# The MLP of a decoder layer as block products: two phases instead of one interleaved stream

## The reference

```python
D_MODEL = 2048; SEQ = 512; D_FF = 4 * D_MODEL
hf = rms_norm(x, norm_mlp[l])
x = x + jnp.square(jax.nn.relu(hf @ w_up[l])) @ w_down[l]
return rms_norm(x, norm_final)
```

## Time and profile before

| | |
|---|---|
| time, median of 3 runs | 2840.79 us (2839.5 to 2841.35) |
| profiled execution, its own time | 2839.88 us |
| its span, first to last instruction | 2838.2 us |
| mean granted TensorE clock | 0.998 |
| instructions | 33822 |

### The profile page before, as it was taken

How to read it: one execution, slowest core, us unless ns; L and a number is a source line. 1 busy time by engine, 2 the same in 40 slices (tenths; PEclk the granted TensorE clock), 3 DMA queues, 4 the chain that set the end, 5 groups by cost and what they waited for, 6 DMA issues and landing times.

```text
span 2838.2 us, 33822 instructions
## 1 busy us (share of the span) xinstructions
PE 2808.7 (99%) x12777; PEld 2321.5 (82%) x12777; DVE 1597.4 (56%) x2058; ACT 1012.1 (36%) x1370; POOL 403.7 (14%) x254
## 2 busy tenths in 40 slices
PE   8999999999999999999999999999999999999998
PEld 7888888888788888888878888888888888888886
DVE  5222245454335556532344577776777777767776
ACT  6222234343232223322344333334333344333334
POOL 1000000000000001000000322332233223313330
PEclk9999999999999999999999999999999999999999
DMA  7323232332333232543212233233223322332232
GB/s 269 104 93 100 89 104 103 103 103 104 104 119 104 74 111 97 190 165 104 89 60 87 77 119 103 91 104 118 90 88 117 118 84 93 118 118 77 101 119 104
DMA packets 132034, 306.27 MB, mean 108 GB/s; under 512 B 7561, under 2 KB 7674, under 8 KB 129530
## 3 DMA queue, kind: packets, MB, share of 16 engines
q1 hardware_dynamic: 130522, 294.80, 31.0%
q10 hardware_dynamic: 1440, 10.49, 0.9%
HBM read 290.58 MB, written 14.68 MB: 108 GB/s over the span
## 4 chain that ended last, share of the span: by engine, by line
PE 97%; DVE 1%; ACT 1%; issue 0%; DMA 0%; SPq 0%; POOL 0%; POOLq 0%; DVEq 0%; ACTq 0%
PE acc L1668 16%; PE acc L1670 16%; PE acc L1669 16%; PE acc L1994 8%; PE acc L1993 8%; PE acc L1992 8%; PE aux L2012 7%; PE aux L2014 7%; PE aux L2016 7%; PE aux L1689 1%; PE aux L1779 1%; PE aux L1762 0%; PE aux L1761 0%; PE aux L1771 0%; PE acc L2034 0%
## 5 line engine op out<-in xcount | busy, mean ns | idle before, releaser
L1013 DVE TENSOR_TENSOR wlo<-raw,whi 128x2048 fp32r<-128x2048 f32 x128 | 293.3, 2291 | 490.9 <-ACT whi L610 489.8
L1668 PE MATMUL acc<-act_hi,whi 128*128 128x512 f32 x1088 | 432.4, 397 | 0.5 <-DVE act_lo L1017 0.5
L1670 PE MATMUL acc<-act_hi,wlo 128*128 128x512 f32 x1088 | 425.0, 391 | 0.0
L1669 PE MATMUL acc<-act_lo,whi 128*128 128x512 f32 x1088 | 424.1, 390 | 0.0
L1446 DVE TENSOR_TENSOR flo<-wide,fhi 128x1024 fp32r<-128x1024 f32 x188 | 257.7, 1372 | 253.2 <-ACT fhi L884 253.2
L610 ACT ACTIVATE whi<-raw 128x2048 fp32r<-128x2048 f32 x128 | 244.5, 1910 | 435.7 <-PE acc L1670 427.4
L1992 PE MATMUL acc<-act_hi,fhi 128*128 128x512 f32 x1024 | 398.7, 389 | 0.0
L1994 PE MATMUL acc<-act_hi,flo 128*128 128x512 f32 x1024 | 398.4, 389 | 0.0
L1993 PE MATMUL acc<-act_lo,fhi 128*128 128x512 f32 x1024 | 398.4, 389 | 0.0
L884 ACT ACTIVATE fhi<-wide 128x1024 fp32r<-128x1024 f32 x188 | 199.4, 1061 | 525.0 <-PE acc L1994 364.8
L2012 PE MATMUL aux<-fhi,P_hi 128*128 128x512 f32 x840 | 326.8, 389 | 0.2 <-DVE xs L1505 0.2
(11 more groups left out here) (313 smaller groups left out, 4159.8 us busy)
## 6 DMA issues: line engine op xcount, KB each, us to landing
raw<-in_w_in SPq DMA_DIRECT2D x80, 1024.0 KB, 5.1
raw<-in_w_up SPq DMA_DIRECT2D x64, 1024.0 KB, 5.3
wide<-in_w_down SPq DMA_DIRECT2D x64, 1024.0 KB, 5.2
raw<-in_w_out SPq DMA_DIRECT2D x16, 1024.0 KB, 5.1
gates_scratch<-gate_out ACTq DMA_DIRECT2D x10, 1024.0 KB, 3.9
raw<-in_w_ckv SPq DMA_DIRECT2D x8, 1024.0 KB, 11.5
xs<-in_x SPq DMA_DIRECT2D x8, 1024.0 KB, 12.8
raw<-in_w_attn_br SPq DMA_DIRECT2D x8, 1024.0 KB, 8.2
```

The source lines that it names most:

```text
L1013: nc.vector.tensor_tensor(wlo[n % 2][:], raw[n % 4][:], whi[n % 2][:].bitcast(F32), ALU.subtract).then_inc(lo_ready, 1)
L1668: nc.tensor.matmul(dst, s_hi, v_hi, start=first, stop=False)
L1669: nc.tensor.matmul(dst, s_hi, v_lo, start=False, stop=False)
L1670: ins = nc.tensor.matmul(dst, s_lo, v_hi, start=False, stop=last)
```

## The change

The MLP is made in two phases, each of blocks with 14 units (`UNITS`), two units per product and seven products per block.

* **Up phase**, 16 blocks (`N_UP`) of 512 features. The 2x2 block product is over halves of 1024 input features, halves of 256 output features and halves of 256 tokens. A unit is 24 matmuls with **256** tokens moving, and a block is 336. The weight mixes are made by POOL, **eight** per block of 128x1024 (`up_mixes`). The input-side sums are made once, ahead of and within block 0 (`mlp_input`, `input_sum`, `low_lo`, `sum_lo`). Products are gathered in PSUM; ACT reads three partial ones out (`product_read`), DVE adds and squares (`hidden`), ACT relus the last (`last_read`), DVE squares it and makes the four sums of the down projection's left operands (`hidden_sum`).
* The seven left operands of a block are split (`operand_hi` on ACT, `operand_lo` on DVE) into three staging tiles and stored to DRAM by SP (`hid_scratch`), 0.5 MB each. All of it is done while the next block's units run.
* **Down phase**, 16 blocks: blocks over 1024 feature rows and 1024 output columns. A unit is 12 matmuls of 512 columns, two units per product. The left operands come back from DRAM, 1 MB per product, double-buffered; eight POOL mixes per block (`down_mixes`). The last block is 8 plain units with 192 matmuls.
* The residual `xs` is stored to DRAM ahead of the MLP and read back into `x_half` at the end of the up phase, since its space is used in between.

Units in all: up 16 x 14 = 224 and down 15 x 14 + 8 = 218, where there were 128 up and 218 down units before. An up unit has 24 matmuls as before, each with half the columns.

The core of the diff:

```diff
-WITH_UP = ("P1", "U", "P2", "P6", "U", "P7", "P5", "U", "P4", "P3", "U")
+UNITS = 14
 RING = 4
+N_UP = 16
+N_BLOCKS = 32
+OPERAND_POS = {"P1": 0, "P4": 1, "P2": 2, "C12": 3, "P5": 4, "P6": 5, "P7": 6, "P3": 8}
...
+        def load_up(slot, b, ready, count):
+            k, f = slot % 2, slot // 2
+            column = (b.first // 2) * 1024 + f * 512 + (b.first % 2) * 256
+            src = w_up_v[:, 8 * k:8 * k + 8, ds(b.turn * (b.per * 512) + column, 256)]
+            sp.wait_ge(ready, count)
...
+        def loads_after_up(b, load):
+            load(0, b.next(), unit_lo, b.of(UNITS, 8))
+            load(1, b.next(), mix_w_ready, b.of(8, 8))
+        def later_loads_after_up(b, load):
+            load(2, b.next(), unit_lo, b.of(UNITS, 10))
+            load(3, b.next(), unit_lo, b.of(UNITS, 12))
...
+        def up_mixes(b):
+            for u in range(2):
+                pool.wait_ge(unit_lo, b.of(UNITS, u + 1))
+                pool.wait_ge(raw_loaded[2], b.of(16, 512 + 16))
+                mixed(nc.gpsimd.tensor_tensor(half_slot(0, u), half_slot(0, u), half_slot(2, u), ALU.subtract))
+                pool.wait_ge(raw_loaded[3], b.of(16, 512 + 16))
+                pool.wait_ge(mix_w_ready, b.of(8, 2 * u + 1))
+                mixed(nc.gpsimd.tensor_tensor(mix[u][:], half_slot(3, u), half_slot(0, u), ALU.subtract))
+            for u in range(2):
+                mixed(nc.gpsimd.tensor_tensor(half_slot(2, u), half_slot(2, u), half_slot(3, u), ALU.add))
+            for u in range(2):
+                pool.wait_ge(unit_lo, b.of(UNITS, 4 + u + 1))
+                pool.wait_ge(mix_w_ready, b.of(8, 4))
+                mixed(nc.gpsimd.tensor_tensor(mix[u][:], half_slot(1, u), mix[u][:], ALU.subtract))
...
+        def before_unit(b, n):
+            if n == 1:
+                hidden(b, "C21")
+            if n == 3:
+                hidden_last(b)
+                hidden_sum(b, "S1")
+                hidden_sum(b, "S2")
+        def behind_unit(b, n):
+            for name in operand_list(b):
+                if OPERAND_POS[name] == n:
+                    operand_lo(b, name)
+            if n == 3:
+                hidden_sum(b, "S3")
+            if n == 5:
+                hidden_sum(b, "S4")
...
+            for m in range(2):
+                bank = up_bank(b, name)[:, 256 * m:256 * (m + 1)]
+                for i in range(4):
+                    k = 4 * u + i
+                    nc.tensor.matmul(bank, w_hi[:, i, cols(m)], x_hi[:, k, :], start=name in UP_FRESH and n % 2 == 0 and m == 0 and i == 0,
+                                     stop=False, skip_group_check=True)
+                    nc.tensor.matmul(bank, w_hi[:, i, cols(m)], x_lo[:, k, :], start=False, stop=False, skip_group_check=True)
+                    ins = nc.tensor.matmul(bank, w_lo[:, i, cols(m)], x_hi[:, k, :], start=False, stop=u == 1 and i == 3,
+                                           skip_group_check=True)
```

More of the change, by code:

```diff
@@ new lines, in down_block, with next_side @@
+        def down_block(b):
+            d = b.first - N_UP
+            sides_free = d % 2 and (not isinstance(b.turn, int) or b.of(1) < N_BLOCKS - 4)
+            i = (d // 2) % 2
+            q = ds(b.turn * 2 + (d // 2 + 2), 1) if sides_free else None
+            def next_side(pi):
+                if sides_free:
+                    load_side(i, q, PRODUCTS[pi], b.of(UNITS, 2 * pi + 2))
+            next_side(0)
+            next_side(1)
+            for slot, lo, pi in ((1, 8, 2), (0, 10, 3), (2, 12, 4), (3, 14, 5)):
+                load_down(slot, b.next(), unit_lo, b.of(UNITS, lo))
+                next_side(pi)
+            next_side(6)
@@ new lines, in _ @@
+        first = Block_no(0, 2, 0)
+        for slot in range(4):
+            load_up(slot, first, lo_ready, G_FF - 3 + slot)
+            for j in {2: (0,), 3: (1, 2, 3)}.get(slot, ()):
+                for m in range(4):
+                    sp.wait_ge(bank_free[m], freed(B_CO + j, m))
+                sp.dma_start(x2_dram[:, :, cols(j, BLK)], xs[:, :, cols(j, BLK)]).then_inc(x2_stored, 16)
+        for p in range(2):
+            up_block(Block_no(0, 2, p))
+        with sp.Fori(1, N_UP // 2 - 1) as t:
+            for p in range(2):
+                up_block(Block_no(t, 2, p))
@@ new lines, in down_block @@
+        def down_block(b):
+            first = isinstance(b.turn, int) and b.of(1) == N_UP
+            chunk = Block_no(0, 2, N_UP - 1)
+            for n in range(UNITS):
+                if first:
+                    before_unit(chunk, n)
+                elif n in (1, 3):
+                    land(b.next(-1), {1: "P4", 3: "P3"}[n])
+                if n in (5, 7, 9, 11, 13):
+                    land(b, PRODUCTS[(n - 5) // 2])
+                unit_split_lo(b, n, True)
+                if first:
+                    behind_unit(chunk, n)
@@ L1611, in left_gain @@
+        last = Block_no(0, 2, N_BLOCKS - 1)
+        for n in range(8):
+            if n in (1, 3):
+                land(Block_no(0, 2, N_BLOCKS - 2), {1: "P4", 3: "P3"}[n])
+            dve.wait_ge(unit_hi, last.of(UNITS, n + 1))
+            nc.vector.tensor_tensor(flo[ring(last, n)][:], half_slot(n // 2, n % 2), fhi[ring(last, n)][:].bitcast(F32),
+                                    ALU.subtract).then_inc(unit_lo, 1)
         def left_gain(m):
             if m == 0:
-                dve.wait_ge(fin_loaded, 16)
+                dve.wait_ge(fin_loaded, 32)
@@ new lines, in down_unit @@
+        def down_unit(b, n):
+            name, u, d = PRODUCTS[n // 2], n % 2, b.first - N_UP
+            i_ = (d // 2) % 2
+            pe.wait_ge(unit_lo, b.of(UNITS, n + 1))
+            if u == 0:
+                if d % 2 == 0 and name in ("P1", "P5"):
+                    h, loads = (0, 4) if name == "P1" else (1, 3)
+                    pe.wait_ge(side_loaded[i_][h], b.turn * (b.per * 4 * loads) + (d // 4 + 1) * 16 * loads)
+                p = PRODUCTS.index(name)
+                if isinstance(b.turn, int) and b.of(1) == N_UP + 1 and p < 2:
+                    pe.wait_ge(dve_read, 4 * N_UP)
+                if p >= 2:
+                    pe.wait_ge(pair_free, b.of(7, p - 1 - 7 * N_UP))
+            a_hi, a_lo = sides[i_][name][:, 0], sides[i_][name][:, 1]
+            w_hi, w_lo = (f[ring(b, n)][:].rearrange("p (k n) -> p k n", k=2) for f in (fhi, flo))
+            for m, bank in enumerate(bank_pair(d % 2, name)):
@@ L2053, in _, with plain_side @@
[L2053 to L2065 removed]
+        def plain_side(m, k):
+            t = sides[1][{(0, 0): "P1", (0, 1): "P2", (1, 1): "P4"}[m // 2, k // 4]] if (m // 2, k // 4) != (1, 0) else side_c12
+            return t[:, 0, k % 4, cols(m % 2)], t[:, 1, k % 4, cols(m % 2)]
```

929 lines of the change are left out of this document (502 added, 427 removed).

## The result

The kernel after takes **2991.5 us** (median of 4 runs, 2990.97 to 2993.32), the kernel before 2840.25 (4 runs, 2839.5 to 2841.35): 1.0533 times as long, 95% interval 1.0515 to 1.0552. It is slower, by 151 us where 84 had been forecast; 2991.5 lies inside the range of 2862 to 3000, near its upper end.

What follows compares the result with a forecast made beforehand. PE's matmuls were taken to bound the kernel before; POOL and DVE delaying each other would make PE wait after the change. Terms -51 + 106 + 20 + 10 = +85 on 2839.9 gave 2924 us, range 2862 to 3000.

Steps and rivals of the forecast that it cites:

- matmuls, 0.120 us apart: Up phase: 5376 matmuls of 256 columns at 0.120 us replace 3072 of 512 at 0.2267, -51.3 us.
- 15 up blocks: Steady up blocks: PE waits 7.1 us per block of 47.4 us; +106 us, bounds +68 to +146.
- start, block 0: Block 0: input differences on DVE alternate with POOL's mixes and delay PE; +20 us, bounds 10 to 30.
- between the phases: Last up to first down block: +6 us for DVE and POOL, +4 for queued stores; +10 us.
- the next thirteen: Down blocks: DVE's lead covers the delay from POOL; 0 us, bounds 0 to 1.5 per block, 21 in all.
- turns: DVE operations with two SBUF inputs and POOL mixes alternate, each waiting out the other; 44 us per up block.
- Squares: DVE's squares in up blocks: counted as waiting for POOL; if free, a block is 0.4 us shorter, 6 in all.
- covered by little: Down blocks: over eight mixes DVE falls back 5.0 us against a lead of 5.7, so no cost.
- Rival 3: Up phase: slot 3's weights land too late for POOL's second mix; 4 us per block, +60, 2984 us; chance 0.14.

Runs made afterwards that it cites:

- narrow: The kernel after with POOL's mixes cut to one column in all blocks but the first, mixed weights left out of the result: 2827.8 us.
- fill: The kernel after with one column of each mix computed and the other 1023 filled with a constant, in all blocks: 2816.1 us.
- queues: The kernel after with down-block weight loads issued ahead of side loads, and x2 and P3 loads behind the first operands' stores between phases: 2973.9 us.
- spread: The kernel after with the fifth to eighth POOL mix of an up block made to wait for later units' splits, same work: 2964.5 us.
- late0: The kernel after with POOL's first mixes held back until block 0's last low input part is done: 3001.7 us.
- combo2: The kernel after with mixes on DVE, SP's loads reordered, block 0's first mixes and sums behind all x2 additions: 2820.35 us, 0.9928 of the kernel before.

## Why the prediction came out as it did

Where the 152 us of the profiled executions (2992.0 against 2839.9) lie, by the prediction's own terms; each is the stretch less what PE wants there at full clock:

| term | forecast | measured |
|---|---|---|
| matmuls, 0.120 us apart | -51.3 | -51.3 |
| 15 up blocks | +106 | +125.5 (15 x 8.37) |
| start, block 0 | +20 | +24 |
| between the phases: the first down block | +10 | +24.5 |
| the next thirteen | 0 | +28.5 |
| sum | +85 | +151 |

So the time came out 67 us above the forecast: 19.5 of them in the up blocks, 4 at the start, 14.5 between the phases, 28.5 in the down blocks. Two terms lie outside their own bounds, the step between the phases (24.5 against at most 21) and the down blocks (28.5 against at most 21); that the total stayed inside the range is partly luck, since the up blocks (at most 146) and the start (at most 30) stayed under theirs. The measured terms add up to within 1 us of the 152, which is closer than they are sharp (the last block of seven products, 1.8 us too long, is in none of them); the start is the least sharp of them (17.9 us idle in 65.9, and about 6 by matmuls at a clock of 0.87; the 48.03 us busy would be some 42 at full clock).

**Right, and shown: turns.** The mechanism is the one forecast: `narrow` cuts the mixes to one column and `fill` keeps their writes without the reads, and in both the up blocks fall to 40.3 us and DVE from 44.2 to 28.2. The 20.9 us from unit 0's split to unit 3's had been worked out as 20.4, and unit 7's split came 13.2 us later (20.9 to 34.1) against 13.0. That the 44 us of turns and DVE's busy 44.2 are the same number is partly luck: the first is 25 of DVE's own and 19 of POOL's, the second 28 of DVE's own and 16 spent beside mixes. Adding instructions up in their order from rows of a kernel that never waited was good to half a microsecond in 21.

**Matmuls.** The 256-column ones come 0.120 us apart, as the earlier trace rows said. By the formula of the Trainium skill, "TensorE: Matmul & The Clock Gate", Back-to-back issue gap, it would be 0.109 and 25 us more of gain; the trace does not agree. That section of the Trainium skill gives the formula for an isolated matmul, which the prediction left out, and about 131 ns at 512 columns for a stream with weight loads; the earlier trace rows have 226.7, so neither holds for this kernel.

**Squares.** They wait too (2.02 us at 1623.56, where one that meets no mix takes 0.69). So the rule of the Trainium skill, "SBUF — State Buffer", Who interferes with whom, that any DVE instruction with two SBUF inputs waits, agrees with the trace, and so does its other half, that POOL instructions which only write don't contend (`fill`).

**Mis-sized: the up block**, 8.4 us for 7.1. Of the 1.3 us too few, 0.5 are hand-overs up to unit 3's split, 0.2 those from there to unit 7's and 0.2 to 0.3 PE's short delays around unit 7: together they make the block of 48.4 us, where 47.4 had been forecast. The other 0.3 are PE's clock. No step of the prediction asked what the 6 us wait, which it had forecast, does to the matmuls behind it. The first 1.7 us of that loss fall where PE would otherwise wait for unit 7; only where the low clock lasts longer does the block grow. The trace bears this out over the 15 blocks: with 14 to 19 slow steps a block takes 48.4 or 48.5 us, with 20 or 21 it takes 48.5 or 48.6, with 26 to 28 it takes 49.2 to 49.4.

**Mis-sized: the step between the phases**, 24.5 us for 10. The place and both causes were named. In `narrow` the first down block takes 56.4 us and the second catches up with 34.0, 14.2 us lost in both; so by this difference about 10 us of the 24.5 are turns, where 6 had been said, and 14 are transfers and what waits for them, where 4 had been said. Stores were said to queue behind the reads, but the length was not worked out. Ten microseconds of the wait, in the kernel after:

```profile
2320.00:2330.00 10.00, 2.66 (x12) 1.88 (x10) 0.00 (x0) 0.00 (x0) 10.00 (x5) 0.79 1.00 424
```

At such a rate 4 MB of x2 and a side of 1 MB are some 12 to 13 us by themselves ahead of a store of 0.5 MB, with other loads not yet done ahead of these. The wait was 20.8.

**Wrong: the down blocks**, 28.5 us for 0. DVE's lead was set at 5.7 us against 5.0 lost, "covered by little", and the mixes were taken to start on time. In every second block they don't: slot 3's weights are issued last in a block, and POOL's second mix waits for them in the blocks that follow side loads (4.2 us in the block of 41.2 shown), so that the turns fall where the lead is already used up. And with mixes on time the cover still fails by 1.2 us: `queues` keeps the turns and takes 39.3 in each block. `narrow` keeps the side loads without the turns and takes 38.1. Of the 28.5 us the side loads' place is 13.2, by `queues`; the other 15, 1.2 a block, go with the turns. The prediction followed the splits alone; what PE waits for in the block of 41.2 is the landing, which stands behind them on DVE:

```profile
PE aux L2281 <- DVE x_half L1814: 2.6, 2, 1.6
```

**Rival 3** (weights too late in the up phase) was not it, but by little: a load of `w_up` landed in 9.5 us instead of 5.3, and neither of POOL's first two mixes waits for one by more than 0.6 us in a block (0.30 in the rows shown). The 11.8 us of slack were all but used up, and in `spread`, with shorter blocks and a later eighth mix, the loads did come late.

**The start** came as said, 24 for 20. `late0` shows 5.2 of its first 11.5 us to be turns; the 6.3 left are the two additions of x2 behind the sums in DVE's order, and `combo2` takes these up.
